# Gate and up weights with eight adjacent rows on each partition, and normalised rows written in the matching column order

## The reference, cut to what matters

```python
D_MODEL = 1024; SEQ = 2048; N_GROUPS = 4; EXP_PER_GROUP = 8; N_EXPERTS = 32; TOP_K = 2; D_FF_EXPERT = 512

x = x + concat(oA, oB) @ W_out            # gated linear attention heads, sliding-window heads
u = rms_norm(x, norm2_w)                  # (2048, 1024)
gp = softmax(u @ w_group + b_group)       # top group of 4
el = (u @ w_router + b_router)            # 32 logits; top 2 of the 8 experts in that group
y  = (silu(xb @ w_gate[e]) * (xb @ w_up[e])) @ w_down[e]   # for the rows xb that chose expert e
x  = x + gate * y                         # summed over a token's two experts
out = rms_norm(x, final_norm_w)
```

## Time and profile before

| | |
|---|---|
| median of 3 runs | 1895.41 us |
| profiled execution | 1894.32 us, span 1892.5 us |
| mean granted TensorE clock | 0.970 |
| TensorE matmul busy | 1774.1 us, 94% |
| TensorE weight load busy | 1270.8 us, 67% |
| VectorE, ScalarE, GpSimd busy | 525.1, 497.3, 297.0 us |
| DMA | 127760 packets, 312.86 MB, 165 GB/s over the span |
| queue of SP (q1) | 112180 packets, 269.87 MB, 40.2% of 16 engines |
| queue of GpSimd (q0) | 15552 packets, 42.61 MB, 8.9% of 16 engines |

### The profile page before, as it was taken

The page is one execution under the profiler, slowest core; times in us unless marked ns, Lnnn a source line. Parts: engine busy times, 40 slices in busy tenths (PEclk is TensorE's granted clock), DMA queues, the critical chain, the costliest instruction groups (busy, mean ns, idle before and its releaser), DMA issues. The chain is left out here.

```text
span 1892.5 us, 28498 instructions
## 1 busy us (share of the span) xinstructions
PE 1774.1 (94%) x10628; PEld 1270.8 (67%) x10629; DVE 525.1 (28%) x1089; ACT 497.3 (26%) x1221; POOL 297.0 (16%) x353
## 2 busy tenths in 40 slices
PE   7999999999999999999973899999999999999980
PEld 4556666566656666566642788888888888888860
DVE  1333234332333324343237211111111111111114
ACT  1434332343334423334320011111111111111114
POOL 0000001000110101101001312222222222222223
PEclk9999999999999999999985999999999999999995
DMA  9411001110111001110013499989999899999969
GB/s 319 96 45 46 12 33 44 44 44 4 41 44 44 37 7 44 44 44 14 31 67 127 145 295 321 321 294 316 311 315 330 269 340 315 312 314 314 309 200 359
DMA packets 127760, 312.86 MB, mean 165 GB/s; under 512 B 10179, under 2 KB 18388, under 8 KB 127732
## 3 DMA queue, kind: packets, MB, share of 16 engines
q1 hardware_dynamic: 112180, 269.87, 40.2%
q0 software_dynamic: 15552, 42.61, 8.9%
HBM read 265.27 MB, written 47.19 MB: 165 GB/s over the span
## 5 line engine op out<-in xcount | busy, mean ns | idle before, releaser
L285 PE MATMUL bank<-w_in_sb,uT 128*128 128x512 f32 (+1 forms) x1024 | 378.3, 523 | 2.4 <-DMA w_in_sb<-w_in_in 2.4
L285 PEld LDWEIGHTS bank<-w_in_sb,uT 128*128 128x128 f32 x1024 | 176.1, 192 | 169.8 <-issue 167.0
L1149 PEld LDWEIGHTS bank<-xT,wts 128*128 128x128 f32 x2048 | 250.5, 192 | 21.5 <-issue 17.2
L1149 PE MATMUL bank<-xT,wts 128*128 128x128 f32 (+2 forms) x2048 | 254.4, 284 | 3.1 <-issue 2.0
L1160 PE MATMUL bank<-xT,wts 128*128 128x128 f32 (+2 forms) x2048 | 247.9, 282 | 0.0
L1160 PEld LDWEIGHTS bank<-xT,wts 128*128 128x128 f32 x2048 | 245.0, 191 | 0.0
L1185 PE MATMUL bank<-wts,hT 128*128 128x512 f32 x512 | 231.7, 595 | 0.0
L433 PE MATMUL bank<-w_out_sb,mixT 128*128 128x512 f32 x512 | 224.1, 596 | 0.8 <-ACT mixT L512 0.8
L433 PEld LDWEIGHTS bank<-w_out_sb,mixT 128*128 128x128 f32 x512 | 96.6, 191 | 116.9 <-issue 116.9
L1238 DVE TENSOR_TENSOR hT<-bank,sg 128x160 f32<-128x160 f32 x128 | 41.6, 325 | 442.1 <-PE bank L1160 442.1
L1185 PEld LDWEIGHTS bank<-wts,hT 128*128 128x128 f32 x512 | 92.2, 190 | 97.6 <-issue 97.6
(11 more groups left out here) (230 smaller groups left out, 1744.1 us busy)
## 6 DMA issues: line engine op xcount, KB each, us to landing
wts<-w_gate_in SPq DMA_DIRECT2D x32, 2048.0 KB, 10.7
wts<-w_up_in SPq DMA_DIRECT2D x32, 2048.0 KB, 9.3
wts<-w_down_in SPq DMA_DIRECT2D x32, 2048.0 KB
x_sb<-x_in SPq DMA_DIRECT2D x17, 512.0 KB, 3.6
w_in_sb<-w_in_in SPq DMA_DIRECT2D x4, 2048.0 KB, 13.1
h_sb<-x_in SPq DMA_DIRECT2D x16, 512.0 KB, 4.6
h_dram<-h_sb SPq DMA_DIRECT2D x16, 512.0 KB, 2.7
v_dram<-v_sb SPq DMA_DIRECT2D x16, 512.0 KB, 2.9
```

Source lines behind the costliest of these rows:

```text
L285: m = pe.matmul(bk[name][:, col:col + hi - lo], uT[:, k, :], w_in[:, k, lo:hi], start=k == 0, stop=k == KD - 1)
L1149: m = pe.matmul(G[m_ % 2][:, 0:w], wg[:, k, m_ * P:(m_ + 1) * P], xT[:, k, 0:w], start=k == 0, stop=k == KD - 1)
```

## The change

The rows of `w_gate`, `w_up`, `w_group` and `w_router` are spread over partitions with eight adjacent rows on a partition (row 8p + k on partition p) in place of rows k x 128 + p. To match, VectorE writes the normalised tile `v2` with its columns permuted: block k of 128 columns holds columns 8p + k, which it reads with a step of eight numbers. The host lays out the norm's weight accordingly. `w_down` keeps its layout.

```diff
-        sp.dma_start(w_r[:, :, 0:NG], A["w_group"][0].rearrange("(k p) n -> p k n", p=P)).then_inc(sem("w_out_loaded"), 16)
-        sp.dma_start(w_r[:, :, NG:NR], A["w_router"][0].rearrange("(k p) n -> p k n", p=P)).then_inc(sem("w_out_loaded"), 16)
+        sp.dma_start(w_r[:, :, 0:NG], A["w_group"][0].rearrange("(p k) n -> p k n", p=P)).then_inc(sem("w_out_loaded"), 16)
+        sp.dma_start(w_r[:, :, NG:NR], A["w_router"][0].rearrange("(p k) n -> p k n", p=P)).then_inc(sem("w_out_loaded"), 16)
...
-            dve.tensor_scalar(v2[:, :], h[:, 1 - par, :], ss[:, 9:10], None, ALU.mult).then_inc(sem("v2_ready"), 1)
+            dve.tensor_scalar(v2[:, :].rearrange("q (k p) -> q k p", p=P), h[:, 1 - par, :].rearrange("q (p k) -> q k p", k=KD),
+                              ss[:, 9:10], None, ALU.mult).then_inc(sem("v2_ready"), 1)
...
-        sp.dma_start(dst, src.rearrange("e (k p) n -> p (e k) n", p=P)).then_inc(sem(f"{pre}{name}_loaded"), 16)
+        rows = "e (k p) n -> p (e k) n" if which == "d" else "e (p k) n -> p (e k) n"
+        sp.dma_start(dst, src.rearrange(rows, p=P)).then_inc(sem(f"{pre}{name}_loaded"), 16)
...
-    a["norm2_t"] = np.ascontiguousarray(a.pop("norm2_w").reshape(KD, P).T)
+    a["norm2_t"] = np.ascontiguousarray(a.pop("norm2_w").reshape(P, KD))
```

## The result

The changed kernel takes **1992.8 us** (median of 4 runs, 1992.1 to 2001.8), the kernel before 1894.9 us (4 runs, 1892.7 to 1896.1): a ratio of 1.0533, with a 95% interval of 1.0515 to 1.0551. It is slower by some 98 us. The prediction said slower, by a mechanism that the trace then showed in the main, but 1958 us with a range up to 1980. The time lies above the range.

The account below looks back on a forecast made before the run. The prediction took TensorE to bound the expert stage, with weight loads and gathers hidden. It summed 1894.3 us profiled + 63 for gather waits + 0.5 for the scaling = 1957.8, said 1958 us, range 1894 to 1980.

Parts of the forecast that it names:

- the merge: Gate and up loads: eight adjacent rows become one 16 KB packet in place of 2 KB ones, some 57,000 packets fewer.
- the turns: Gate load beside row gather: DMA engines alternate between queues by packet, not by byte, making the gather 4.3 to 4.7 us later.
- The term of width 128: Expert chunks of width 128: TensorE waits 4.2 us for the late gather in 15 chunks, +63 us, ends 35 and 68.
- the term of width 144: Nine expert chunks of width 144: gather 2.0 to 2.6 us later against 2.0 us of slack, 3 us in all.
- The chunks of width 160: Five expert chunks of width 160: the gather, with 3.6 us of slack, is down before the gate load starts; no loss.
- While TensorE waits nothing hides behind it: Expert stage: later scatter, gather and down load shift by the same amount as each wait, so the chunks' terms add.
- The scaling: VectorE's scaling of a tile, read with a step of 8 words: 1.283 us in place of 0.743, +0.54 us paid once.
- The cover: Steady iterations: 1.4 us between products ready on VectorE and TensorE's start hides the slower scaling, except at the last tile.
- Rival 1: Gather before the transposes: nothing moves, as loads keep 2 KB packets or large ones are cut finely; 1895 us, chance 0.29.
- Rival 2: Gate load beside the gather: large packets are cut at 4 KB, +6 us in 15 chunks, 1901 us, chance 0.09.
- Rival 3: Gate load starts sooner and meets the gather in all chunks, +27 us on top, 1985 us, chance 0.10.
- Rival 4: Faster: would need a wait of TensorE for a transfer in the expert stage, and there is none; chance 0.07.

Follow-up runs that it names:

- experiment 1: The changed kernel with the up weights back in the old row order (2 KB packets), gate load keeping 16 KB packets; 1990.3 us, ratio 1.050.
- experiment 2: The changed kernel with the gate weights back in the old row order (2 KB packets), up load keeping 16 KB packets; 1896.6 us, ratio 1.0001.
- experiment 4: The changed kernel with one more wait on SP, so the gate load is issued only when the next rows' gather has landed; 1901.6 us, ratio 1.0035.
- experiment 6: The changed kernel with the gate load issued as two DMAs, even and odd rows, so its packets are 2 KB; 1895.6 us, ratio 1.0000.
- experiment 7: The kernel before (2 KB packets, old row order) with three idle GpSimd passes ahead of each gather in the loop; 2001.0 us, ratio 1.0573.
- experiment 5: The change with two or four adjacent rows on a partition, packets of 4 or 8 KB; 1904.2 us (ratio 1.0043) and 1938.9 us (1.0226).

## Why the prediction was partly right, point by point

**Right: the bound, the merge, the turns.** TensorE bounded the stage, and a slower transfer made it wait only for what went beyond its slack. The gate load's eight rows become one packet of 16 KB (57342 packets fewer, 57,000 said). Turns are by packet: 88 to 88. Experiments 1, 2, 4 and 6 put the whole loss on the one meeting that the prediction named, gate load and gather. The landing in the 15 chunks of width 128, said at 11 to 12 us, is 11.2 to 11.5.

**The term of width 128: right, a little high.** Said 15 waits of 4.0 to 4.5 us, 4.2 taken, 63 us. The trace has 15 of 3.26 to 3.56 us, 51.4 us in all. The packets have the sizes of the working (0.61 us for 16 KB, where 0.62 to 0.68 was taken; 0.15 us for 4 KB, where 0.17 was): 8 x (0.15 + 0.61) = 6.1 us. The landing moved by 3.8 us (7.5 to 11.3), and 3.8 less the 0.27 us of slack is 3.5.

**Wrong: the term of width 144, mis-sized.** "Meets the last 1.0 us of the gather, some 3 to 4 packets", 0.3 us a chunk and 3 us in all, left in the range. Measured: nine waits of 0.9 to 2.4 us, 14.3 us. The gathers of these nine chunks landed after 10.7 us on average (10.1 to 11.6) where 9 to 9.6 was said, against 6.9 us before: 3.8 us later, as much as in width 128. What was mis-sized is the overlap of the two transfers. The step put the start of the gate load about 4 us behind its issue, at 1244.1. In the trace of before GpSimd's queue and SP's sent this from 1243.2 to 1244.1:

```profile
q0 software_dynamic: 79, 0.29, 77.9%
q1 hardware_dynamic: 43, 0.09, 25.1%
```

The load had started at 1243.2, 3.2 us behind its issue. The chunk was an odd one besides: its gate load is issued 2.01 us behind the gather, and in all nine of the kernel after it is 1.65 us. There the large packets begin 1.65 + 3.4 = 5.1 us behind the gather's issue, and so meet the last 1.9 us of a gather of 7.0 us, not the last 1.0: at 0.255 us a turn some 7 of its 8 packets on the last engine, not 3 to 4. One such gather was issued at 1425.53 and landed 11.5 us later. From 1430.5 us, where the large packets begin, to 1437.2, by queue:

```profile
q1 hardware_dynamic: 155, 2.28, 81.0%
q0 software_dynamic: 158, 0.50, 18.6%
```

GpSimd's queue still has 0.50 MB to send. At most 0.13 MB of it is the gather of the tail (128 quarter rows of 1 KB), so at least 0.37 MB of the row gather's 0.52 MB is left, some 5.6 packets of 4 KB an engine on average and more on the last engine. Width 144 thus differs from width 128 in its slack, and hardly in the delay. The chunks of width 160 lost nothing, as said.

**Wrong: a term that wasn't there, the clock.** "While TensorE waits nothing hides behind it" was said, and nothing of what comes after the wait: what a wait does to the clock was put at nothing, without a reason. Busy time grew by 31.0 us; experiment 7 shows 25.2 us of the same with 2 KB packets and waits alone. This term is what put the time outside the range: 1957.8, less 11.6 for the width 128, plus 14.3 for the width 144 is 1960.5; plus 31.0 it is 1991.5, against the 1992.3 us of the profiled execution.

**The scaling: small, and once.** Said 1.283 us a tile, 1.14 measured, between the two rows that bounded it. By the rule of the Trainium skill (VectorE: DVE Perf Modes, What auto-detection actually checks) as the prediction read it, the time would have stayed at 0.743 us; the trace disagrees. By the lines of 16 bytes of the Trainium skill (SBUF — State Buffer, Door 1) every element would have paid. The kernels of experiment 5 tell the two rules apart. They read with steps of two and of four words:

```profile
L722 DVE TENSOR_SCALAR v_sb<-h_sb,ss 128x1024 f32<-128x1024 f32 x16 | 11.9, 742 | 2.2 <-POOL ss L736 2.2
...
L722 DVE TENSOR_SCALAR v_sb<-h_sb,ss 128x1024 f32<-128x1024 f32 x16 | 18.5, 1156 | 2.2 <-POOL ss L736 2.2
```

The outermost dimension is even in both, and in the change. A step of two words (8 bytes) costs nothing, one of four (16 bytes) as much as one of eight: the pass is slow from where each 16 bytes hold only one of the numbers read. That fits the lines and not the rule of the outermost dimension alone; that it is the lines, and not something else that begins at a step of four words, is not shown. The cover held: the steady iteration's transposes start at 540.20 us (540.33 before), and only the last tile's wait grew:

```profile
995.49 1.07 PE L280 MATMUL bank<-ident,v_sb 128*128 128x128 f32 x8 [4.21 <-DVE v_sb L719]
```

4.21 us in place of 3.81: +0.40, where 0.54 was said.

**The rivals.** Rival 1 (nothing moves) fell with the packet count. Rival 2 (a cut at 4 KB) fell with the 16.4 KB of a packet; by the Trainium skill (DMA: Bandwidth & Descriptors, SWDGE vs HWDGE vs iDMA), where a packet has preferably at most 4096 bytes and the engine changes queues at its end, the change would have lost no more than the kernel with 4 KB packets. That one cost 0.43%, 8 us, where rival 2 had said 6; the change cost 98. Rival 3 (the gate load starts sooner) gave the nearest time, 1985 us, for the wrong reason: the start of the gate load stayed 3.3 to 3.6 us behind its issue (3.2 to 3.7 in most chunks before), chunks of width 160 didn't wait, and the loss in width 144 came of an overlap that had been there before and was reckoned too small. Rival 4 had no wait to win back, and experiments 4 and 6 are not faster either.

## What to carry to other kernels

A long run makes a load's packet large, and a queue beside it that moves something small and urgent then waits one such packet for each of its own: look for the transfer with the least slack that is under way at the same time, and keep the packets of its neighbour small, or issue the neighbour behind it. A wait put on a TensorE that was never idle may cost up to half as much again in clock, so price it at more than its length. Where the cost hangs on how long two transfers overlap, read in several chunks where the packets of each begin: here 1.9 us of overlap in place of 1.0 turned 3 us into 14.

## What the runs showed of the hardware

- Two DMA queues with work for the same engines alternated packet for packet, 88 to 88, with packets of 16.4 and 3.9 KB; a run of 16 KB that is contiguous on both sides went as one packet, although its address comes from a register.
- A stretch of 4.0 us with such a mix moved 445 GB/s, against 387 GB/s with 2 KB packets alone, and SP's queue moved its 269.87 MB in 724 us of 16 engines (36.4% of 1990.4) in place of 761 us (40.2% of 1892.5). Nobody waited for the gain.
- A gate load with nothing beside it began 1.0 us behind its issue (all 31 of experiment 4); issued beside GpSimd's scatter, 3.3 to 3.6 us behind it (29 of 31 in the kernel after).
- TensorE's granted clock fell to 0.50 about 1 us after the restart behind a wait of 3.4 us (in other chunks at once) and stayed there for some 3 us. Over the 24 waits (65.7 us) matmul time grew by 31.0 us; over 12 waits of at most 0.6 us it grew by 0.8.
- Reading with a step of 8 words took 1.14 us in place of 0.743 for 1024 float32 numbers a partition, on VectorE with one source; a step of 4 words took 1.16 us, a step of 2 words 0.742 us.
